# Gate and up tiles: high and low part of x side by side, two of three products in one matmul

## What is computed

```python
def rms_norm(x, w):
    y = x * lax.rsqrt(jnp.mean(x * x, axis=-1, keepdims=True) + EPS)
    return y * w

def swiglu(h, w_in, w_out):              # w_in (1024, 2 x 2816), w_out (2816, 1024)
    gate, up = jnp.split(h @ w_in, 2, axis=-1)
    return (jax.nn.silu(gate) * up) @ w_out

x = x + 0.5 * swiglu(rms_norm(x, norm_w), w_in, w_out)
```

## Time and profile before

| | us |
|---|---|
| median of 3 runs | 2027.57 (2027.02 to 2030.83) |
| profiled execution, its own time | 2027.62 |
| span of that execution, first to last instruction | 2025.80 |
| TensorE busy, 15374 matmuls | 1914.1 |
| VectorE busy | 1201.7 |
| ScalarE busy | 901.2 |
| mean granted TensorE clock | 0.975 |

### The profile page before, as it was taken

One profiled execution on the slowest core, in us unless ns is written; L12 is line 12 of the kernel. 1 busy time (PEld: TensorE's weight loads), 2 busy tenths in 40 slices (PEclk: granted clock), 3 DMA queues, 4 the chain that ended last, 5 costly groups with the idle time before them and its releaser, 6 DMA issues.

```text
span 2025.8 us, 36529 instructions
## 1 busy us (share of the span) xinstructions
PE 1914.1 (94%) x15374; PEld 1862.8 (92%) x15374; DVE 1201.7 (59%) x1330; ACT 901.2 (44%) x1180; POOL 147.3 (7%) x169
## 2 busy tenths in 40 slices
PE   6999999999999998999499999999998899999997
PEld 6999998898999998999499999999998858999997
DVE  5555676766455556555754655565555685555555
ACT  4443554565453444433344533344443474344333
POOL 2020100131010003000210100010001001010001
PEclk9999999999999998999789999999999899999998
DMA  6654353434445553554334455545553312435452
GB/s 230 229 186 171 135 185 125 154 129 146 146 148 185 186 186 141 193 182 176 118 105 153 160 180 177 183 167 187 185 177 141 146 43 105 170 143 177 179 184 104
DMA packets 45706, 324.90 MB, mean 160 GB/s; under 512 B 5165, under 2 KB 5301, under 8 KB 6688
## 3 DMA queue, kind: packets, MB, share of 16 engines
q1 hardware_dynamic: 44352, 316.56, 43.8%
q0 software_dynamic: 1248, 6.77, 1.0%
HBM read 322.25 MB, written 1.06 MB: 160 GB/s over the span
## 4 chain that ended last, share of the span: by engine, by line
PE 86%; DVE 7%; ACT 3%; POOL 2%; issue 1%; DMA 0%; POOLq 0%; SPq 0%; DVEq 0%; ACTq 0%
PE PS L533 26%; PE PS L535 26%; PE PS L534 26%; ACT w_hi L1170 2%; DVE w_lo L1725 2%; DVE xT_lo L1746 1%; PE PS L675 1%; PE PS L693 1%; POOL both L448 1%; DVE x L1788 1%; PE PS L1090 1%; PE PS L1126 1%; PE PS L1109 0%; PE PS L797 0%; PE PS L567 0%
## 5 line engine op out<-in xcount | busy, mean ns | idle before, releaser
L1725 DVE TENSOR_TENSOR w_lo<-raw,w_hi 128x2048 fp32r<-128x2048 f32 x299 | 687.3, 2299 | 457.7 <-ACT w_hi L1170 457.6
L1170 ACT ACTIVATE w_hi<-raw 128x2048 fp32r<-128x2048 f32 x299 | 571.9, 1913 | 815.5 <-PE PS L535 815.0
L533 PE MATMUL PS<-xT_hi,w_hi 128*128 128x256 f32 x2704 | 780.1, 289 | 46.6 <-DVE xT_lo L1746 30.3
L534 PE MATMUL PS<-xT_lo,w_hi 128*128 128x256 f32 x2704 | 770.6, 285 | 0.0
L535 PE MATMUL PS<-xT_hi,w_lo 128*128 128x256 f32 x2704 | 770.2, 285 | 0.0
L533 PEld LDWEIGHTS PS<-xT_hi,w_hi 128*128 128x128 f32 x2704 | 524.7, 194 | 56.0 <-issue 41.3
L534 PEld LDWEIGHTS PS<-xT_lo,w_hi 128*128 128x128 f32 x2704 | 524.9, 194 | 0.7 <-issue 0.5
L535 PEld LDWEIGHTS PS<-xT_hi,w_lo 128*128 128x128 f32 x2704 | 524.6, 194 | 0.0
L533 PE MATMUL PS<-h_hi,w_hi 128*128 128x256 f32 x1280 | 367.3, 287 | 15.4 <-DVE x L1788 15.4
L535 PE MATMUL PS<-h_hi,w_lo 128*128 128x256 f32 x1280 | 364.9, 285 | 0.0
L534 PE MATMUL PS<-h_lo,w_hi 128*128 128x256 f32 x1280 | 364.8, 285 | 0.0
(11 more groups left out here) (279 smaller groups left out, 1978.4 us busy)
## 6 DMA issues: line engine op xcount, KB each, us to landing
raw<-weights SPq DMA_DIRECT2D x299, 1024.0 KB, 4.8
arena<-mems POOLq DMA_DIRECT2D x5, 1024.0 KB, 7.8
x<-x_in SPq DMA_DIRECT2D x2, 512.0 KB, 4.4
out<-x SPq DMA_DIRECT2D x4, 256.0 KB, 2.5
both<-toep POOLq DMA_DIRECT2D x1, 512.0 KB, 4.2
arena<-toep POOLq DMA_DIRECT2D x1, 512.0 KB, 6.0
con<-consts SPq DMA_DIRECT2D x1, 498.0 KB, 9.5
arena<-dtw SPq DMA_DIRECT2D x1, 256.0 KB, 11.6
```

The source lines that it names most:

```text
L533: pe.matmul(out, lh, rh, start=start, stop=False, skip_group_check=True)
L534: pe.matmul(out, lh, rl, start=False, stop=False, skip_group_check=True)
L1170: act.activation(w_hi[:, slot, :], raw[:, raw_slot, :], ACT.Copy).then_inc(hi_ready, 1)
L1725: dve.tensor_tensor(w_lo[:, slot, :], raw[:, raw_slot, :], w_hi[:, slot, :], ALU.subtract).then_inc(lo_ready, 1)
```

## The change

xT_hi and xT_lo become two views of one tensor, chunk by chunk side by side, so that high and low part of a chunk are 512 adjacent columns. In gate and up tiles w_hi is then multiplied with both at once, one matmul of 512 columns into a whole bank: columns 0 to 255 hold hi by hi, columns 256 to 511 hi by low. The product of w_lo and xT_hi is a matmul of 256 columns onto the first half. A tile has 32 matmuls instead of 48 and fills two banks, one for each half of its features; gate tiles use banks 4 and 5, up tiles 6 and 7, every time. So TensorE waits for the banks of the tile before (gate_taken, up_taken). ScalarE copies the low halves of the two banks to SBUF, VectorE adds the first halves from PSUM, and then multiplies by the row, from SBUF now. Two new waits on up_taken guard banks 6 and 7 where the memory statistics use them. All other projections and the down tiles stay as they are.

```diff
-        xT_hi = sb("xT_hi", [P, KC, S], F32R)
-        xT_lo = sb("xT_lo", [P, KC, S], F32R)
+        xT = sb("xT", [P, KC, 2, S], F32R)
+        xT_hi, xT_lo = xT[:, :, 0, :], xT[:, :, 1, :]
...
-                proj(n0, n0 % SPL, 4, "x", False, at.norm - 1)
+                def paired(n, slot, bank, fresh=None, mid=None):
+
+                    pe.wait_ge(lo_ready, n + 1)
+                    for part in range(2):
+                        for k in range(KC):
+                            if fresh is not None and part == 0:
+                                pe.wait_ge(xlo_ready, fresh * KC + k + 1)
+                            w = k * 256 + part * P
+                            pe.matmul(PS[:, bank + part, :], w_hi[:, slot, w:w + P],
+                                      xT[:, k].rearrange("p a b -> p (a b)"), start=k == 0, stop=False,
+                                      skip_group_check=True)
+                            last = pe.matmul(PS[:, bank + part, 0:S], w_lo[:, slot, w:w + P], xT_hi[:, k, :],
+                                             start=False, stop=k == KC - 1, skip_group_check=True)
+                        if mid is not None and part == 0:
+                            mid()
+                    last.then_inc(tile_used, 1)
+
+                paired(n0, n0 % SPL, 4, at.norm - 1)
                 statistic_sums(double)
-                proj(n0 + 1, (n0 + 1) % SPL, 5, "x", False, None, lambda: statistic_row(double))
+                paired(n0 + 1, (n0 + 1) % SPL, 6, None, lambda: statistic_row(double))
...
-                    proj(n, (n0 + 2) % SPL, 4 + 2 * p, "x", False)
+                    pe.wait_ge(gate_taken, it * 2 + (f0 + s + 1))
+                    paired(n, (n0 + 2) % SPL, 4)
                     if mid:
                         mid()
-                    proj(n + 1, (n0 + 3) % SPL, 5 + 2 * p, "x", False)
+                    pe.wait_ge(up_taken, it * 2 + (f0 + s + 1))
+                    paired(n + 1, (n0 + 3) % SPL, 6)
...
+                def gate_low(used, p):
+                    act.wait_ge(tile_used, used)
+                    act.activation(gate[:, p], PS[:, 4:6, S:2 * S], ACT.Copy).then_inc(gate_side, 1)
+
+                def up_low(used, p, free=None):
+                    act.wait_ge(tile_used, used)
+                    if free is not None:
+                        act.wait_ge(hlo_ready, free)
+                    act.activation(hid[:, p], PS[:, 6:8, S:2 * S], ACT.Copy).then_inc(up_side, 1)
...
+                if at.norm - 1 == DOUBLE:
+                    act.wait_ge(acc_ready, at.stat + 1)
+                gate_low(n0 + 1, 0)
                 statistic_row(rrow, at.norm - 1 == DOUBLE)
                 silu(0, 0)
+                up_low(n0 + 2, 0)
                 next_split()
...
+                    gate_low(it * 6 + (r + 1), p)
                     ahead(0)
-                    silu((1 + s) % 2, it * 2 + (1 + s))
+                    silu(p, i)
+                    up_low(it * 6 + (r + 2), p, None if first else it * 2 + (f0 + s))
                     ahead(1)
...
-                def scaled_gate(n, p):
-                    dve.wait_ge(tile_used, n + 1)
-                    dve.tensor_tensor(gate[:, p], PS[:, 4 + 2 * p, :].rearrange("p (a b) -> p a b", a=2), row2,
-                                      ALU.mult).then_inc(silu_in, 1)
+                def scaled_gate(p, i):
+                    dve.wait_ge(gate_side, f0 + i + 1)
+                    dve.tensor_tensor(gate[:, p], gate[:, p], PS[:, 4:6, 0:S], ALU.add).then_inc(gate_taken, 1)
+                    dve.wait_ge(gate_taken, f0 + i + 1)
+                    dve.tensor_tensor(gate[:, p], gate[:, p], row2, ALU.mult).then_inc(silu_in, 1)
...
+                def product(p, i):
+                    dve.wait_ge(up_side, f0 + i + 1)
+                    dve.tensor_tensor(hid[:, p], hid[:, p], PS[:, 6:8, 0:S], ALU.add).then_inc(up_taken, 1)
+                    dve.wait_ge(up_taken, f0 + i + 1)
+                    dve.tensor_tensor(hid[:, p], hid[:, p], row2, ALU.mult).then_inc(up_scaled, 1)
                     dve.wait_ge(up_scaled, f0 + i + 1)
                     dve.wait_ge(silu_done, f0 + i + 1)
                     dve.tensor_tensor(hid[:, p], hid[:, p], gate[:, p], ALU.mult).then_inc(hidden, 1)
```

More of the change, by code:

```diff
@@ L296, in program @@
         prep = sem("prep")
+        gate_side = sem("gate_side")
+        up_side = sem("up_side")
+        gate_taken = sem("gate_taken")
+        up_taken = sem("up_taken")
         silu_in = sem("silu_in")
@@ L639, in ffn @@
                     pe.wait_ge(macc_ready, 2)
+                    pe.wait_ge(up_taken, f0 + 9)
                     for j in range(4):
@@ L646, in ffn @@
                     pe.wait_ge(mdiag_ready, 1)
+                    pe.wait_ge(up_taken, f0 + 11)
                     for i in range(2):
@@ L1252, in ffn, with pair @@
                 next_split()
+                if at.norm - 1 == DOUBLE:
+                    act.wait_ge(acc_ready, at.stat + 1)
+                gate_low(n0 + 1, 0)
                 statistic_row(rrow, at.norm - 1 == DOUBLE)
                 silu(0, 0)
+                up_low(n0 + 2, 0)
                 next_split()
                 hidden_hi(0, 0)
-                def pair(it, s):
+                def pair(it, s, first=False):
                     r = n0 + 2 + 3 * s
@@ L1262, in ahead @@
                         loop_split(None, n % SPL, n % RAW, it * (6 // RAW) + (n // RAW + 1), it * 6 + (r + j + 1))
+                    p, i = (1 + s) % 2, it * 2 + (1 + s)
+                    gate_low(it * 6 + (r + 1), p)
                     ahead(0)
-                    silu((1 + s) % 2, it * 2 + (1 + s))
+                    silu(p, i)
+                    up_low(it * 6 + (r + 2), p, None if first else it * 2 + (f0 + s))
                     ahead(1)
-                    hidden_hi((1 + s) % 2, it * 2 + (1 + s))
+                    hidden_hi(p, i)
                     ahead(2)
-                for a, b in ((0, 2), (2, 4)) if f0 == 0 else ((0, 5),):
+                pair(0, 0, True)
+                pair(0, 1)
+                for a, b in ((1, 2), (2, 4)) if f0 == 0 else ((1, 5),):
                     with act.Fori(a, b) as it:
@@ L1272, in ffn @@
                             pair(it, s)
-                    if f0 == 0 and a == 0:
+                    if f0 == 0 and a == 1:
                         act.wait_ge(mstat_landed, 32)
@@ L1867, in ffn @@
                 dve.wait_ge(rrow_ready, at.stat)
-                scaled_gate(n0, 0)
-                product(n0, 0, 0)
+                scaled_gate(0, 0)
+                product(0, 0)
                 if double:
@@ L1881, in pair @@
                     p = (1 + s) % 2
-                    scaled_gate(it * 6 + r, p)
+                    scaled_gate(p, it * 2 + (1 + s))
                     ahead(0)
-                    product(it * 6 + r, p, it * 2 + (1 + s))
+                    product(p, it * 2 + (1 + s))
                     ahead(1)
```

## The result

| | before | after |
|---|---|---|
| median, us | 2029.2 | 2011.49 |
| all runs, us | 2027.02 to 2031.29 (4 runs) | 2006.32 to 2014.87 (4 runs) |
| profiled execution, us (span) | 2027.62 (2025.8) | 2014.87 (2013.1) |
| mean granted clock | 0.975 | 0.975 |

The ratio is 0.9911, interval 0.9885 to 0.9936: 17.7 us less, where 28.5 were forecast (1999.1; the range was 1974 to 2020). The profiled execution of the kernel after is the slowest of its four, so its span is not the one to compare.

The account below looks back on a forecast made before the run. TensorE, busy 94% of the span and carrying 86% of the chain, was taken as the bound. 2037 pairs x 14 ns = 28.5 us, with added work hidden, came off 2027.6 us: 1999.1 us, range 1974 to 2020.

Parts of the forecast that it names:

- What bounds it: Whole kernel: TensorE, busy 94% of the span, so only its own stream or added waits before it move the end.
- rival A: Gate and up tiles: 512-column matmul takes 220 to 232 ns, 8 to 20 less per pair, centre 1999 us; chance 0.60.
- Pair 346 ns, 14 less: Gate and up tiles: 226 ns for the 512-column matmul plus 120 for w_lo's, against 360 ns for three matmuls before.
- The prediction is wrong if the w_lo matmul's spacing changes: Gate and up tiles: a failure sign; spacing after the 256-column matmul on w_lo was to stay at 120 ns.
- 2037 pairs gain: Gate and up tiles: of 2112 pairs, all gain but 32 + 32 at stage starts and 11 at 1.2 GHz.
- At the lower clock nothing is gained: Up tiles at 1.2 GHz: 256 columns already take 213 ns, exactly 256 / 1.2, so some 11 pairs gain nothing.
- Copies, additions and waits hidden: Feed-forward loops: added ScalarE copies (0.65 us), VectorE additions (0.69 us) and bank waits cost no time; three tiles take 16.83 us.
- Stage end "costs 0": Last down tile of a stage: h_lo perhaps 0.2 us late, but TensorE waits for VectorE's x anyway, so cost 0.
- B: Gate and up tiles: weight load is the limit, 512 columns hide it at 216 ns; 48.9 us less, 1978.7 us; chance 0.20.
- C: Gate and up tiles: excess comes by column, 512 columns take 240 ns, gain 0 to 5 us, 2025 us; chance 0.10.
- D: Gate and up tiles: 512-column matmul paced above 240 ns, so slower; 2048 us at 250 ns, up to 2415 us; chance 0.10.

Follow-up runs that it names:

- r1_three: Changed kernel with three matmuls of 256 columns again instead of one of 512 and one of 256 in gate and up tiles; 2026.58 us, ratio 0.9996.
- r1_only512: Changed kernel without the w_lo product in gate and up tiles, leaving sixteen 512-column matmuls per tile; 1767.84 us, ratio 0.8718.
- r1_halfload: Changed kernel with the w_lo matmuls of gate and up tiles loading only 64 of 128 weight columns; 2001.84 us, ratio 0.9872.
- r2_group: Changed kernel with each half's eight 512-column matmuls first, then its eight of 256 on w_lo; 2009.44 us, ratio 0.9907.

## Why the prediction was right in its sign and over a third off in its size

- **What bounds it: right; rival A's mechanism: right only for wide matmuls among themselves.** r1_three shows that nothing but the wide matmul moved the time, and r1_only512 that its own pace is 226.7 ns, as A had it. In the changed kernel it takes 236 ns on average and a pair gains 14.0 us / 1920 = 7.3 ns, both outside what A allowed (220 to 232, 8 to 20).
- **"Pair 346 ns, 14 less": the term that was mis-sized.** It added the two paces as each has it among its own kind. In alternation the pair takes 353.6 ns in 106 of 119 tiles and 346.7 in 13: 5.64 to 5.66 us a tile where 5.54 was forecast. Over the 120 tiles that is 692.1 - 678.1 = 14.0 us, where 120 x 16 x 14 ns = 26.9 were counted; the down tiles give 0.4 more. The trace of before has no pairs of this kind, but it held a hint that I didn't use: the 71 steps of the earlier trace rows, all alike, are not 117 ns each but between 113 and 122, so the excess is no fixed price per matmul.
- **"The prediction is wrong if the w_lo matmul's spacing changes": it did change**, to 113 to 120 ns, mean 117. It is a gain, but the mark rightly told that the sum of two paces doesn't hold.
- **"2037 pairs gain".** For the 117 or so outside the 120 tiles 1.6 us were counted, and no gain shows: a stage's first two tiles sum to 110.5 to 111.3 us over six stages, against 110.0 before. But r1_three, with TensorE's old stream, has 107.7, so this sum varies by more than the term. The prediction also gave the first stage the 4.04 us wait for GpSimd's sums; in the trace of before that one is 1.8 us.
- **At the lower clock nothing is gained: right.** TensorE's timeline in an up tile at 1.2 GHz, as the earlier trace rows, shows 0.42 + 0.22 = 0.64 us for a pair at granted clock 0.50, which is 768 / 1.2:

```profile
786.17 0.63 PE L630 MATMUL PS<-xT,w_hi 128*128 128x512 f32 x1
786.59 0.41 PE L633 MATMUL PS<-xT,w_lo 128*128 128x256 f32 x1
786.81 0.63 PE L630 MATMUL PS<-xT,w_hi 128*128 128x512 f32 x1
```

- **Copies, additions and waits hidden: right**, by r1_three and the two waits above. The group of three tiles takes 85.33 / 5 = 17.07 us, not 16.83.
- **Stage end "costs 0": right.** TensorE and VectorE where the second stage's last down tile ends, as the earlier trace rows:

```profile
1308.98 0.28 PE L539 MATMUL PS<-h_hi,w_lo 128*128 128x256 f32 x1
1310.88 0.39 PE L537 MATMUL PS<-h_hi,w_hi 128*128 128x256 f32 x1 [1.62 <-DVE x L1832]
```

```profile
1305.39 0.69 DVE L1908 TENSOR_TENSOR h_lo<-arena,h_hi 128x512 fp32r<-128x512 f32 x1
1308.19 2.29 DVE L1769 TENSOR_TENSOR w_lo<-raw,w_hi 128x2048 fp32r<-128x2048 f32 x1 [2.12 <-ACT w_hi L1195]
```

  h_lo ends at 1306.1, 5.6 us after the up tile (ScalarE's copy of it starts at 1300.49; 5.8 were forecast), and the stand that follows is 1.9 us where it was 2.15, still set by the last split.
- **The rivals.** B (load is the limit) would have shown 216, C (excess by column) 240, D above 240: the 226.7 of wide matmuls among themselves rules out all three as mechanisms. In numbers the kernel came out between A and C. The Trainium skill, "TensorE: Matmul & The Clock Gate", section "Wait — 56ns, not 53.3ns?", gives B's 216 at 512 columns; the bf16 matmul of the earlier trace rows agrees, no fp32r run here does.
- **What stays open.** The tile sums account for 14.4 us, exactly repeated in three profiles; the medians differ by 17.2 to 19.6. The 3 to 5 us left lie outside the loops and were not attributed; there the granted clock varies between profiles. The stage that takes 184.3 us in the profile of before takes 188.7, 182.4 and 182.7 in three of the change, at a granted clock of 0.91 in the longest and 0.94 in the three others. The last down tile of the last stage takes 9.3 us before, at 0.82, and 7.8 at 1.00 in all three of the change, but also in r1_three. So the total came out at three fifths of the forecast gain, and the part that the prediction is about, the pairs in the loops, at half; the difference between the two is luck, as far as the runs show. Nor is it settled how load and stream make the cycles, or what decides which one a tile falls into; r1_halfload only shows that the load has a part.

## What to carry to other kernels

Don't price an interleaved stream of matmuls by adding up what each kind takes among its own: measure the sequence, or put it into runs of equal length, here two by two. Here one wide matmul in place of two paid about 12 ns with the matmuls two by two, and about 7 ns with wide and narrow in turn, at full clock only. Before grouping, look at places where the stream is paced by its inputs: what filled the gaps there will stand behind them. Merging products at the price of a copy and an addition elsewhere was free here, with VectorE and ScalarE busy 59% and 44% of the span and two tiles of slack. And measure a tile from start to start: from end to end, its time changes with the length of its last matmul.

## What the hardware showed that I had not expected

- Alternating fp32r matmuls of 512 and 256 columns don't run at the sum of their paces but mostly in a cycle of three pairs (353.6 ns per pair, 106 of 119 tiles); the faster 346.7 ns per pair holds only in 13 tiles, nearly all at a stage's start.
- A turn from 256 columns to 512 costs 27 to 28 ns over the next five to eight wide matmuls (r1_only512, r2_group); a turn to 256 gives 8 back, as the first matmuls of 256 go at 113 and 119 ns before 120 is reached (r2_group).
- Loading 64 instead of 128 weight columns for the short matmul speeds up the long one beside it, from 233 to 241 down to 229 ns (r1_halfload).
